# Two waits moved in the tail of the routed experts: when the lower rows are gathered, and when the next projection's first weights are split

## The reference

```
for layer in range(2):
    h, hc = h + g1*mixer(norm(h)), ...           # layer 0: Fourier + neighbourhood attention
                                                 # layer 1: retention
    tok = concat(norm(hc), norm(h))              # 512 tokens in layer 0, 256 in layer 1
    gate = top-2 of 16 experts per token
    f = sum_e gate[:, e] * ((silu(tok @ w1[e]) * (tok @ w3[e])) @ w2[e])
    hc, h = hc + g2c*f[:n_c], h + g2*f[n_c:]
x = rmsnorm(h)      # then the second block: rms_norm(x) @ w_in_2 ...
```

## Time and profile before

| what | us |
|---|---|
| median of 3 runs | 1778.05 (1777.85 to 1780.46) |
| the profiled execution, its time | 1780.59 |
| the profiled execution, its span | 1778.7 |
| TensorE busy | 1690.3 (95%) |
| VectorE busy | 1150.8 (65%) |
| ScalarE busy | 1007.5 (57%) |

### The profile page before, as it was taken

One profiled execution on the slowest core, in us unless ns is written; L12 is line 12 of the kernel. 1 busy time (PEld: TensorE's weight loads), 2 busy tenths in 40 slices (PEclk: granted clock), 3 DMA queues, 4 the chain that ended last, 5 costly groups with the idle time before them and its releaser, 6 DMA issues.

```text
span 1778.7 us, 30129 instructions
## 1 busy us (share of the span) xinstructions
PE 1690.3 (95%) x12270; PEld 1446.3 (81%) x12270; DVE 1150.8 (65%) x1587; ACT 1007.5 (57%) x1334; POOL 69.4 (4%) x66
## 2 busy tenths in 40 slices
PE   5999999899999999999999799999989999999898
PEld 4787666888898868889879588888869998897688
DVE  5432864799898873343355698989965676544564
ACT  4322753488888875224353578888854563453462
POOL 0000000000000100000000010000100000100100
PEclk9999999999999999999999899999999999999999
DMA  8646205799999944223663399999964444363512
GB/s 328 217 126 257 114 14 218 306 376 411 402 412 399 376 191 178 95 95 143 235 239 143 136 382 397 410 404 406 392 235 166 173 175 152 85 225 142 161 53 72
DMA packets 52558, 419.81 MB, mean 236 GB/s; under 512 B 16980, under 2 KB 18132, under 8 KB 30048
## 3 DMA queue, kind: packets, MB, share of 16 engines
q1 hardware_dynamic: 26416, 364.55, 52.0%
q0 software_dynamic: 8304, 31.64, 5.7%
q10 hardware_dynamic: 17728, 22.02, 3.6%
HBM read 398.22 MB, written 19.97 MB: 235 GB/s over the span
## 4 chain that ended last, share of the span: by engine, by line
PE 81%; DVE 7%; DMA 5%; ACT 3%; issue 3%; POOL 1%; SPq 0%; ACTq 0%; DVEq 0%; POOLq 0%
PE ps L754 48%; PE ps L899 16%; PE ps L715 5%; DMA ring<-w_all 3%; PE ps L738 2%; PE ps L908 1%; DMA y_d<-arena 1%; DVE w_lo L2314 1%; PE ps L1153 1%; PE ps L1142 1%; PE ps L1168 1%; PE ps L915 1%; PE ps L1427 1%; PE ps L761 1%; DMA arena<-y_d,tok_row 1%
## 5 line engine op out<-in xcount | busy, mean ns | idle before, releaser
L2314 DVE TENSOR_TENSOR w_lo<-ring,w_hi 128x1024 fp32r<-128x1024 f32 x384 | 453.0, 1221 | 53.0 <-ACT w_hi L1652 51.4
L1652 ACT ACTIVATE w_hi<-ring 128x1024 fp32r<-128x1024 f32 x384 | 395.9, 1056 | 106.3 <-PE ps L899 60.0
L754 PE MATMUL ps<-XT_lo,arena_r 128*128 128x256 f32 (+1 forms) x1712 | 386.2, 300 | 6.3 <-DVE ring_r L2166 3.9
L754 PEld LDWEIGHTS ps<-XT_lo,arena_r 128*128 128x128 f32 x1712 | 283.1, 190 | 22.2 <-issue 7.9
L899 PE MATMUL ps<-w_hi,x_hi 128*128 128x256 f32 (+1 forms) x768 | 248.7, 324 | 8.0 <-DVE w_lo L2314 4.7
L899 PE MATMUL ps<-w_lo,x_hi 128*128 128x256 f32 (+1 forms) x768 | 244.4, 318 | 0.0
L899 PE MATMUL ps<-w_hi,x_lo 128*128 128x256 f32 (+1 forms) x768 | 244.3, 318 | 0.0
L754 PE MATMUL ps<-arena_r 128*128 128x512 f32 (+1 forms) x656 | 231.5, 361 | 7.1 <-DVE arena_r L2486 3.8
L2166 DVE TENSOR_TENSOR ring_r<-ring,arena_r 128x1024 fp32r<-128x1024 f32 x96 | 114.0, 1223 | 110.8 <-ACT arena_r L1552 110.5
L754 PE MATMUL ps<-XT_lo,ring_r 128*128 128x256 f32 x640 | 182.1, 285 | 0.0
L899 PEld LDWEIGHTS ps<-w_hi,x_hi 128*128 128x128 f32 x768 | 145.8, 190 | 26.6 <-issue 9.3
(11 more groups left out here) (368 smaller groups left out, 2678.4 us busy)
## 6 DMA issues: line engine op xcount, KB each, us to landing
ring<-w_all SPq DMA_DIRECT2D x172, 2048.0 KB, 9.6
y_d<-arena ACTq DMA_DIRECT2D x30, 512.0 KB, 9.8
arena<-toep_d POOLq DMA_DIRECT2D x16, 384.0 KB, 11.9
arena<-rpb ACTq DMA_DIRECT2D x16, 192.0 KB, 3.9
xtok_d<-arena ACTq DMA_DIRECT2D x6, 512.0 KB, 3.1
hT<-h SPq DMA_DIRECT2D x2, 1024.0 KB, 6.2
arena<-cb_d POOLq DMA_DIRECT2D x1, 1536.0 KB, 12.3
arena<-cc_d POOLq DMA_DIRECT2D x1, 959.0 KB, 6.9
```

The source lines that it names most:

```text
L754: last = nc.tensor.matmul(out, a, b, start=(first and i == 0), stop=(final and i == 2))
L1652: nc.scalar.activation(w_hi[:, q], slot(b, "p (q c) -> p q c", q=4)[:, q], ACT.Copy).then_inc(hi_rdy, 1)
L2314: nc.vector.tensor_tensor(w_lo[:, q], slot(base + n, "p (q c) -> p q c", q=4)[:, q], as_f32(w_hi[:, q]), ALU.subtract).then_inc(*split_sig ...
```

## The change

1. Layer 0 only: the lower gathers wait for `f_u1` of the last expert (its w1 products are finished) instead of `f_x` of the last expert (its rows are turned). In layer 1 the count waited for is the same as before (`2 * EXPERTS` is `EXPERTS * (layer + 1)` there).
2. Layer 0: both engines split quarters 0 to 3 after chunks 4, 5, 6, 7.
3. Layer 1: ScalarE splits quarters 0 to 3 after the squares of chunks 3, 4, 5, 6 (none ahead of the table load), VectorE after the additions of chunks 4, 5, 6, 7 (none ahead of chunk 0).

```diff
@@ gather(layer), GpSimd
-                pool.wait_ge(f_x, EXPERTS * (layer + 1))
+                pool.wait_ge(*((f_u1, EXPERTS) if layer == 0 else (f_x, 2 * EXPERTS)))
                 pool.wait_ge(y_st[layer][1], 112)
@@ routed(layer), ScalarE
-                if layer == 1:
-                    for p in range(2):
-                        z_split(p)
                 table(ACT.Sqrt)
                 for m in range(KT):
                     act.wait_ge(*((f_cT, (KT - 1) * layer + m + 1) if m < KT - 1 else (res_done, 2 * layer + 2)))
                     norm_square(2 * layer + 2, m)
-                    if layer == 0 and m in (2, 3, 4, 5):
-                        ret_split(m - 2)
-                    if layer == 1 and m in (1, 3):
-                        z_split(2 + m // 2)
+                    if layer == 0 and m >= 4:
+                        ret_split(m - 4)
+                    if layer == 1 and 3 <= m < 7:
+                        z_split(m - 3)
                 norm_roots(layer)
@@ routed(layer), VectorE
                 if layer == 1:
                     last_lo()
-                    z_split(0)
...
                     last.then_inc(f_cT if m < KT - 1 else res_done, 1)
-                    if layer == 0 and m in (3, 5, 6, 7):
-                        ret_split((3, 5, 6, 7).index(m))
-                    if layer == 1 and m in (1, 3, 5):
-                        z_split(1 + m // 2)
+                    if layer == 0 and m >= 4:
+                        ret_split(m - 4)
+                    if layer == 1 and m >= 4:
+                        z_split(m - 4)
```

## The result

The changed kernel takes 1782.35 us (median of 22 runs, 1776.87 to 1786.94), the kernel before 1777.49 us (22 runs, 1772.34 to 1783.8) on the same chip. The ratio is 1.0028, with a 95% interval of 1.0019 to 1.0038: slower by 5.0 us (3.4 to 6.8). The forecast was +3.7 us with a range of -1.8 to +7.2. The profiled execution has a span of 1783.6 us against 1778.7; its time of 1785.49 us lies 3.1 us above its median, as the one before with 1780.59 does.

What follows compares the result with a forecast made beforehand. TensorE, busy 95% of the span, and the chain through layer 0's gathers, block load, splits and norm were taken as the bound. Layer 0's +7.3 and layer 1's -3.6 gave +3.7 us: 1781.8 us, range 1776.3 to 1785.2.

Steps and rivals of the forecast that it cites:

- Gathers: Layer 0's tail: lower gathers start at about 616.4 instead of 606.22, so the last upper one lands 1.3 us late.
- the rival by which the later gathers cost nothing: Layer 0: DMA engines, not GpSimd, set the landing, at 631 to 632 as now; sum -0.2 us; chance 0.14.
- The rival with all gathers at 1.96 us: Layer 0: gathers are the bound, costing another 1.8 us there; sum +5.5 us, slower; chance 0.10.
- Split 0: Layer 0: ScalarE's first split of the next projection's block stands behind square 4, at 642.0 against 640.02: +2.0 us.
- The clock term: Layer 0's chunk phase: TensorE at half clock for the first 3 to 4 us, +1.6 us, bounds 0 and 2.3.
- Rounds: Layer 0: ScalarE's split, VectorE's split, chunk and square in series, 3.63 us a round; reciprocal +2.8 us.
- the last sum's half clock: Layer 0: last sum of squares at half clock after three rounds of little TensorE work, +0.9 us, bounds 0 and 0.9.
- Layer 0 together: Sum of layer 0's terms, 2.0 + 1.6 + 2.8 + 0.9: +7.3 us; without the clock +4.8.
- Layer 1: Moved splits end the waits for the block ahead of the chunks: -4.5 us, plus 0.9 for the clock, -3.6.
- Square 7 -4.5: Layer 1: square of chunk 7 done at 1317.7 instead of 1322.15, the sums and projection moving with it: -4.5 us.
- Clock half-charged, +0.9, bounds 0 and 1.8: Layer 1: a clock fall would cost the sums of squares 1.8 us; half of it charged.
- the likeliest case: Whole kernel: the forecast's own case, chance 0.46, +1.9 (one clock term off) to +5.6 us.

Runs made afterwards that it cites:

- e6: Changed kernel plus filler products in layer 0 ahead of the tiles and the last two sums of squares: 1775.94 us, 0.0 against the kernel before.
- e10: Changed kernel with e4's ranges, e6's fillers ahead of the tiles and e5's fillers, gathers still late: 1772.73 us, -3.0 against the kernel before.
- e3: Kernel before with only layer 1's splits moved: 1774.12 us, -2.7 against the kernel before.
- e4: Changed kernel with ScalarE's splits of layer 0 one chunk earlier, after squares 3 to 6: 1776.95 us, -0.7 against the kernel before.
- e7: e3 with layer 0's splits as in e4 and the early gathers: 1772.88 us, -3.2 against the kernel before.
- e9: Kernel before with only the later lower gathers, plus e6's fillers ahead of layer 0's tiles: 1777.61 against 1776.54 us, difference 0.0.
- e8: e7 with e5's fillers in layer 1: 1771.46 us, -4.4 against the kernel before.
- e5: e3 plus three fillers ahead of each of the last three of layer 1's first eight sums of squares: 1771.37 against 1775.69 us, -3.7.

## Why the prediction was right where it was

All on the scale of before (1.66 us added):

- **Gathers.** The first lower one was forecast at 616.4 and came at 615.87, the last upper one at 627.3 and 627.01; the eight calls took 9.94 us together, forecast 9.76. The last one landed at 633.0 (forecast 633.1), so the rival by which the later gathers cost nothing, to be decided by a landing by 632, is out. The last tile ended at 635.57 (forecast 635.8), but not by the way forecast: `last_hi` started at 629.23 + 1.66 = 630.89, a little sooner than before and not at 632.0 to 632.4, and the tile followed from the third upper gather and VectorE's order. That the number fits all the same is in part luck. TensorE's end of the last expert came 3.1 us sooner (3.8), and this bought nothing, as forecast. The rival with all gathers at 1.96 us is refuted by the first row of the timeline. The estimate of 3.2 us for one gather, which the prediction takes from the Trainium skill, "DMA: Bandwidth & Descriptors", section "Anatomy of one DMA — SWDGE (gpsimd) path", is not borne out either: the one on the chain took 5.98 us, with eight issued in a row.
- **Split 0.** Forecast at 642.0 plus 1.6 for the clock. In e6, at full clock, it starts at 640.58 + 1.73 (that run's offset) = 642.31; in the full change at 644.16. The clock term is 1.85 us.
- **Rounds.** 3.65 us (forecast 3.63); reciprocal 13.17 us after split 0 in e6 (13.1), 13.95 in the full change, where the last sum's half clock adds 0.8 (0.9). Undoing the equal places of the two engines takes this to 9.54 us in e10.
- **Layer 0 together:** +7.8, forecast +7.3.
- **Layer 1** is the term that was mis-sized: -3.6 was forecast, the profiled execution has -0.4. It has three parts. "Square 7 -4.5" is what e3 shows (-4.45), but in the profiled execution it was -3.3, because the block came 1.05 us after the squares were ready for it. "Clock half-charged, +0.9, bounds 0 and 1.8" was too little: the stretch from square 7 to the projection is 5.59 us before, 7.24 after, 7.27 in e3 and 8.61 in e4, so a fall costs 1.7 to 3.0 us when it comes, beyond the upper bound in e4. It came in these three and not in e6 (5.58) and e7 (7.63, but with full clock and the unexplained wait), which have the same order in layer 1 and no filler there. Over these five the clock costs 1.3 us on average. The remaining 1.3 us of the shortfall, the longer wait for the last expert's w2, stands ahead of everything that was edited there.

The longest of these falls, TensorE's row of e4:

```profile
1322.00 6.16 PE L761 MATMUL ps<-XT,cst 128*128 128x256 f32 x16
```

So +7.8 and -0.4 stand in the profiled execution for +7.3 and -3.6; what lies ahead of the first tail is 1.7 us shorter and what lies between and behind the tails 0.8, neither of them edited: 4.9 us of span, and +5.0 by the medians. The sign and the likeliest case (+1.9 to +5.6) held. The 1.3 us that the forecast lacks are no more than the interval of the result leaves open (3.4 to 6.8 holds 3.7). Layer 0's 0.5 and the 0.9 by which e3's run (-2.7) stays behind -3.6 would make them up, but e3's own interval (-4.6 to -0.5) holds -3.6 as well: this division is argued, not shown. And that one profiled execution adds up to the median's +5.0 is luck, since layer 1 alone lies anywhere from 34.9 to 39.9 us in the executions with the move and without fillers there.

**What stays open.** The tail's trace gives fillers 2.6 us in e6 and 0.6 in e9, the runs 5.0 and 3.6. Part of that is layer 1's fall that did not come in e6. Behind layer 1, from the projection's start to the end, the executions with fillers take 446.1 to 448.4 us and those without 449.0 to 451.5. Most of this goes with the clock: what it lacks to 1.00 there, summed over the whole stretch, is 1.7 to 1.8 us in e8, e9 and e10 (446.1 to 446.9 us), 3.4 in e3, e4, e5 and e6 (448.0 to 449.9) and 5.1 to 5.5 in the others (450.7 to 451.5). As e5 and e6 have fillers and e3 and e4 have none, fillers in the tails and the clock hundreds of microseconds later need not be cause and effect; with one profiled execution of each it can be chance. That was not tested.

## What to carry to other kernels

When two engines split a piece in turn and both also work on a chain of chunks, put the first engine's share one chunk ahead of the second's: the same work at equal places cost 3.65 us a round, one ahead 1.92. Moving a wait out of one engine's way can leave TensorE with thin work elsewhere; count what stands behind that stretch at half clock, and try a few filler products there before giving up the move (here worth 1.7 us on the products of chunks 0 to 3). A change of several parts should be run part by part: here one of three was worth -2.7 us and was buried under the other two.

## What the hardware showed that I had not expected

**The clock fell after thin work as well as after idle time.** In the kernel after, the rounds with 1.06 us of TensorE work in 3 us (648 to 651) were followed by 0.50, and in layer 1 a stretch of 1.54 in 3 us (e3) by 0.58; with fillers that made it 2.68 in 3 us (e5) the clock stayed at 1.00. The amount of work alone does not decide it: in the 3 us up to square 7 TensorE worked 1.81 us in e3 and 1.81 in e6, and the next 3 us had 0.62 in e3 and 1.00 in e6.

**How long a gather holds GpSimd seems to go by what VectorE does beside it.** In the kernel after, e6, e9 and e10 the eight calls repeat within 0.02 us: 1.05, 1.97, 1.38, 0.94 and 1.58, 1.17, 0.94, 0.94. The 1.97 us one (615.56) lies beside VectorE's uninterrupted splits; the last two lie where VectorE idles (622.92 + 0.15 to 627.28), and the fourth (619.52) mostly beside instructions that read one operand from PSUM. The Trainium skill, "SBUF — State Buffer", section "Who interferes with whom", says that a VectorE instruction with two SBUF inputs contends with a GpSimd instruction that reads SBUF, and one with at most one SBUF input, outside its 2-port modes, does not. The trace agrees in part: the slow calls all lie beside splits, which have two SBUF inputs, but so does the first one (614.21), which took 1.05 us. Against 0.94 the hold came to 0.1 to 1.0 us, never to the 1.22 us of a whole split. The cause was not tested by an experiment of its own.
